# Down product of the feed-forward blocks: one step per two groups, four row tiles deep, and gate, up, gate, two down units, up as the order of the work

## The reference

```python
def swiglu(hn, w_ffn_in, w_ffn_out):
    a, b = jnp.split(hn @ w_ffn_in, 2, axis=-1)
    return (jax.nn.silu(a) * b) @ w_ffn_out
...
ff = swiglu(rmsnorm(h, norm_ffn_pre[l]), w_ffn_in[l], w_ffn_out[l])
h = h + rmsnorm(ff, norm_ffn_post[l])
```

## Time and profile before

| | |
|---|---|
| time, median of 3 runs | 1864.49 us (1863.72 to 1864.56) |
| time of the profiled execution | 1863.81 us |
| its span, first to last instruction | 1862.0 us |
| mean granted PE clock | 0.994 |
| PE busy | 1815.3 us, 97% |
| PE weight loads busy | 1626.4 us, 87% |
| DVE busy | 1335.6 us, 72% |
| ACT busy | 813.3 us, 44% |
| POOL busy | 152.8 us, 8% |
| HBM traffic | 84 GB/s over the span |

### The profile page before, as it was taken

How to read it: one execution, slowest core, us unless ns; L and a number is a source line. 1 busy time by engine, 2 the same in 40 slices (tenths; PEclk the granted TensorE clock), 3 DMA queues, 4 the chain that set the end, 5 groups by cost and what they waited for, 6 DMA issues and landing times.

```text
span 1862.0 us, 28319 instructions
## 1 busy us (share of the span) xinstructions
PE 1815.3 (97%) x11226; PEld 1626.4 (87%) x11226; DVE 1335.6 (72%) x1825; ACT 813.3 (44%) x1031; POOL 152.8 (8%) x97
## 2 busy tenths in 40 slices
PE   9999999999999999999999999999999999999996
PEld 8898989889898888988887989988898888989896
DVE  7567566753736538357678888888898778898887
ACT  5666676532322333333443333334545753343332
POOL 2000000000000000000001222220000001222210
PEclk9999999999999999999999999999999999999998
DMA  4111111132122222112412222223476312322321
GB/s 184 35 65 60 45 45 46 60 111 102 46 90 79 90 96 73 69 68 91 161 69 91 91 101 102 90 103 96 112 187 175 122 68 93 112 90 92 108 95 46
DMA packets 25989, 170.29 MB, mean 91 GB/s; under 512 B 2736, under 2 KB 5040, under 8 KB 6320
## 3 DMA queue, kind: packets, MB, share of 16 engines
q1 hardware_dynamic: 24176, 156.51, 23.5%
q0 software_dynamic: 1728, 12.58, 3.3%
HBM read 154.40 MB, written 2.10 MB: 84 GB/s over the span
## 4 chain that ended last, share of the span: by engine, by line
PE 80%; DVE 13%; issue 4%; ACT 3%; POOL 0%; DVEq 0%; ACTq 0%; POOLq 0%
PE psum L675 25%; PE psum L677 24%; PE psum L676 24%; DVE w_lo L1889 2%; DVE acc L2150 2%; DVE wx_lo L2481 1%; DVE normed L1906 1%; PE psum L826 1%; PE psum L877 1%; PE psum L872 1%; ACT w_hi L1276 1%; DVE h L1996 1%; PE psum L797 1%; ACT X_hi L1276 0%; DVE M_lo L2467 0%
## 5 line engine op out<-in xcount | busy, mean ns | idle before, releaser
L675 PE MATMUL psum<-X_hi,w_hi 128*128 128x512 f32 (+2 forms) x1392 | 467.6, 336 | 20.0 <-DVE gate_in L2549 10.9
L676 PE MATMUL psum<-X_lo,w_hi 128*128 128x512 f32 (+2 forms) x1392 | 457.9, 329 | 0.0
L677 PE MATMUL psum<-X_hi,w_lo 128*128 128x512 f32 (+2 forms) x1392 | 457.9, 329 | 0.0
L1889 DVE TENSOR_TENSOR w_lo<-w_raw,w_hi 128x2048 fp32r<-128x2048 f32 x121 | 294.9, 2438 | 59.6 <-ACT w_hi L1276 59.3
L675 PEld LDWEIGHTS psum<-X_hi,w_hi 128*128 128x128 f32 x1392 | 262.9, 189 | 54.5 <-DVE gate_in L2549 13.9
L1276 ACT ACTIVATE w_hi<-w_raw 128x2048 fp32r<-128x2048 f32 x133 | 253.5, 1906 | 119.8 <-PE psum L677 119.8
L676 PEld LDWEIGHTS psum<-X_lo,w_hi 128*128 128x128 f32 x1392 | 263.6, 189 | 25.6 <-issue 2.4
L677 PEld LDWEIGHTS psum<-X_hi,w_lo 128*128 128x128 f32 x1392 | 263.2, 189 | 23.5
L675 PE MATMUL psum<-M_hi,w_hi 128*128 128x512 f32 (+2 forms) x376 | 141.6, 377 | 0.0
L676 PE MATMUL psum<-M_lo,w_hi 128*128 128x512 f32 (+2 forms) x376 | 141.2, 376 | 0.0
L677 PE MATMUL psum<-M_hi,w_lo 128*128 128x512 f32 (+2 forms) x376 | 141.0, 375 | 0.0
(11 more groups left out here) (352 smaller groups left out, 4034.3 us busy)
## 6 DMA issues: line engine op xcount, KB each, us to landing
w_raw<-in_units SPq DMA_DIRECT2D x140, 1024.0 KB, 4.8
w_lo<-w_raw POOLq DMA_DIRECT2D x12, 1024.0 KB, 7.0
...
```

What stands on the lines that cost most here:

```text
L675: nc.tensor.matmul(dst, w2[0], x2[0], start=first, stop=False, skip_group_check=True)
L676: nc.tensor.matmul(dst, w2[0], x2[1], start=False, stop=False, skip_group_check=True)
L677: m = nc.tensor.matmul(dst, w2[1], x2[0], start=False, stop=last, skip_group_check=True)
L1889: v.tensor_tensor(lo, w_raw[at.ring(j)][:, :], as_f32(hi), ALU.subtract).then_inc(w_lo_ready, 1)
```

## The change

Groups 1 to 10 lose their own down unit. Each pair (0 and 1, 2 and 3, up to 8 and 9) gets one down step of two units of a new kind "E": 4 row tiles of 512 columns, 4 strips each of 12 matmuls 128x512. The four row tiles are the two groups' `M` slots, read as one. Only the last group keeps its "D" unit. The units are laid out in HBM in the new order. PE's order over two groups is now gate, up, gate, both down units, up (`period`); ffn1 has whole units in that order, and ffn9 has gate, up, gate, up, both down units. The tables `FF_BANKS` and `FF_REACH` name the PSUM bank of each strip and how far back the strip that last used it lies; PE waits for that one. The products that need `t4_lo` and `t3_lo` wait for them inside the first seven of a period. On DVE, `u2` and `u3` of a seven now stand ahead of the split of the next unit, and ACT makes `M_hi` between its two copies of a gate's first strip. The last hidden pair goes to `wx_hi` and `wx_lo`, free by then.

```diff
-STRIPS = {"P": 2, "R": 4, "D": 8, "S": 3}
+STRIPS = {"P": 2, "R": 4, "E": 4, "D": 8, "S": 3}
...
+FF_BANKS = {
+    "ffn0": (4, 5, 0, 1),
+    "ffn1": (2, 3, 6, 4, 5, 0, 1, 2, 3, 6, 4, 5, 0, 3, 1, 2),
+    "ffn": tuple((j + 3) % 7 for j in range(20)),
+    "ffn9": tuple((j + 3) % 7 for j in range(20)),
+}
+def reach():
+    last, far, s = {6: 3}, {}, 0
+    for phase in ("ffn0", "ffn1", "ffn", "ffn", "ffn", "ffn9"):
+        for j, bank in enumerate(FF_BANKS[phase]):
+            far[phase, j] = min(far.get((phase, j), 99), s - last[bank] if bank in last else 6)
+            last[bank] = s
+            s += 1
+    return far
+FF_REACH = reach()
 def plan():
...
-        ("ffn1", "PPDPPD"),
-        ("ffn", "SSDSSD" * 3),
-        ("ffn9", "SSDSSD"),
+        ("ffn1", "PPPEEP"),
+        ("ffn", "SSSEES" * 3),
+        ("ffn9", "SSSSEE"),
         ("ffn_end", "D"),
...
-            return (j + 2) % 7
+            return FF_BANKS[self.phase.removesuffix("_2")][j]
         return (self.turn + j) % self.depth * max(1, 4 // self.depth)
+    def before(self, j):
+        return self.strip(j) + 1 - (FF_REACH[self.phase.removesuffix("_2"), j] if self.depth == 7 else self.depth)
...
-            def two(i):
-                at = Place("ffn" + tag, i, 6, 28, 2)
-                for m in range(2):
-                    k = FIRST7 + 2 * i + m + 1
-                    first_sums(at, 3 * m + 1, index7(n, k, 0))
-                    first_sums(at, 3 * m + 2, index7(n, k, 1))
...
+            def period(i):
+                at = Place("ffn" + tag, i, 6, 20, 2)
+                k = FIRST7 + 2 * i
+                for j, (kk, c) in ((0, (1, 0)), (3, (1, 1)), (4, (2, 0)), (5, (2, 1))):
+                    first_sums(at, j, index7(n, k + kk, c))
+            loop(pool, 3, period)
...
-            def down(at, j, s, i, slot):
...
-                unit(at, j, s, "D", SEQ, lambda k, a, b: (M_hi[:, slot, k, :], M_lo[:, slot, k, :]))
-            def seven(at, j, s, idx):
+                m = seq_of(*(x[:, :, :, :].rearrange("p a b c -> p (a b) c") for x in (M_hi, M_lo)))
+                for c in range(2):
+                    unit(at, j + c, s + 4 * c, "E", SEQ, m)
...
+                if first:
+                    pe.wait_ge(t_sums.sem, t_sums.at("t4_lo", n))
                 product(r3, added_to, 0, sum_x(1), False, True, c7_pe.step("P6"))
                 taken(1)
+                if first:
+                    pe.wait_ge(t_sums.sem, t_sums.at("t3_lo", n))
...
+            def period(at, k):
+                seven(at, 0, 0, index7(n, k, 0), True)
+                seven(at, 1, 3, index7(n, k, 1))
+                seven(at, 2, 6, index7(n, k + 1, 0))
+                down(at, 3, 9, base + k)
+                seven(at, 5, 17, index7(n, k + 1, 1))
...
-            two(Place("ffn1" + tag, depth=6), 1)
-            pe.wait_ge(t_sums.sem, t_sums.at("t3_lo", n))
-            loop(pe, 3, lambda i: two(Place("ffn" + tag, i, 6, 28, 7), FIRST7 + 2 * i))
-            two(Place("ffn9" + tag, depth=7), FF_PAIRS - 2)
+            at = Place("ffn1" + tag, depth=7)
+            for j in range(3):
+                whole(at, j, 2 * j)
+            down(at, 3, 6, base + 1)
+            whole(at, 5, 14)
+            loop(pe, 3, lambda i: period(Place("ffn" + tag, i, 6, 20, 7), FIRST7 + 2 * i))
+            at = Place("ffn9" + tag, depth=7)
+            for j in range(4):
+                seven(at, j, 3 * j, index7(n, FF_PAIRS - 2 + j // 2, j % 2))
+            down(at, 4, 12, base + FF_PAIRS - 2)
...
+            def pair_and_gate(at, k, up_next, down_next):
+                strips(at, -1)
+                sums_hi(at, -1, index7(n, k, 1))
+                split_hi(at, -1)
+                gate(at, 0, k, lambda: hidden(base + k - 1, slot(up_next)))
+                strips(at, 2)
+                sums_hi(at, 0, index7(n, k + 1, 0))
+                split_hi(at, 0)
+                takes(at, 3, index7(n, k, 1), up_in, lambda: gated(k))
+                strips(at, 5)
+                if down_next:
+                    split_hi(at, 1)
+                else:
+                    sums_hi(at, 1, index7(n, k + 1, 1))
+                    split_hi(at, 1)
+                gate(at, 6, k + 1, lambda: hidden(base + k, slot(up_next + 1)))
+                strips(at, 8)
+                split_hi(at, 2)
+            def period(at, k):
+                pair_and_gate(at, k, 0, True)
+                gated(k + 1)
+                strips(at, 12)
+                sums_hi(at, 3, index7(n, k + 1, 1))
+                split_hi(at, 3)
+                strips(at, 16)
+                sums_hi(at, 4, index7(n, k + 2, 0))
+                split_hi(at, 4)
+                takes(at, 17, index7(n, k + 1, 1), up_in)
...
+            def wholes(at):
+                hidden_lo(base, *slot(0))
+                for which in ("b12", "t1", "t2", "t4"):
                     token_sums(which)
-                add_down(at, 4, range(3))
+                gates_in(at, 0)
+                split_lo(at, 0)
+                gates(base + 1)
+                token_sums("t3")
+                for t, (name, scale) in enumerate((("t1", 1.0), ("t2", -1.0), ("t4", -1.0))):
+                    token_lo(t, name, scale)
+                ups(at, 2, base + 1)
                 split_lo(at, 1)
-                hidden_lo(i, 1)
-                add_down(at, 4, range(3, 6))
-                token_sums("t4")
-                add_down(at, 4, range(6, DT))
-                token_sums("t3")
+                hidden_lo(base + 1, *slot(1))
+                gates_in(at, 4)
                 split_lo(at, 2)
-                gate_up(at, 3, 12, i + 1, between=lambda: [token_lo(t, name, scale) for t, (name, scale) in
-                                                           enumerate((("t1", 1.0), ("t2", -1.0), ("t4", -1.0)))])
+                gates(base + 2)
+                add_down(at, 6, range(4))
+                split_lo(at, 3)
+                add_down(at, 6, range(4, 6))
                 sums_of(at, 4, index7(n, FIRST7, 0))
+                add_down(at, 6, range(6, DT))
+                sums_lo(at, 4, index7(n, FIRST7, 0))
+                split_lo(at, 4)
+                sums_of(at, 5, index7(n, FIRST7, 1))
+                ups(at, 14, base + 2)
                 dve.wait_ge(t_high.sem, t_high.at("t3_hi", n))
                 v.tensor_tensor(late_half(X_lo), T3_raw, as_f32(late_half(X_hi)), ALU.subtract).then_inc(*t_sums.step("t3_lo"))
-                sums_lo(at, 4, index7(n, FIRST7, 0))
-                add_down(at, 16, range(3))
-                split_lo(at, 4)
-                sums_of(at, 5, index7(n, FIRST7, 1))
-                add_down(at, 16, range(3, 6))
-                hidden_lo(i + 1, 0)
-                sums_lo(at, 5, index7(n, FIRST7, 1))
-                add_down(at, 16, range(6, DT))
...
+            def pair_and_gate(at, k, up_next, down_next):
+                g, u, g2 = index7(n, k, 0), index7(n, k, 1), index7(n, k + 1, 0)
+                sums_lo(at, -1, u)
+                chain(at, 0, g, gate_in)
+                split_lo(at, -1)
+                corner22(at, 0, g, gate_in)
+                hidden_lo(base + k - 1, *slot(up_next))
+                sums_of(at, 0, g2)
+                gate_corners(at, 0, k)
+                sums_lo(at, 0, g2)
+                chain(at, 3, u, up_in)
+                split_lo(at, 0)
+                corner22(at, 3, u, up_in)
+                gated(k)
+                if not down_next:
+                    sums_of(at, 1, index7(n, k + 1, 1))
+                prod(at, 3, k)
+                if not down_next:
+                    sums_lo(at, 1, index7(n, k + 1, 1))
+                chain(at, 6, g2, gate_in)
+                split_lo(at, 1)
+                corner22(at, 6, g2, gate_in)
+                hidden_lo(base + k, *slot(up_next + 1))
+                gate_corners(at, 6, k + 1)
+            def period(at, k):
+                u2, g3 = index7(n, k + 1, 1), index7(n, k + 2, 0)
+                pair_and_gate(at, k, 0, True)
+                split_lo(at, 2)
+                gated(k + 1)
+                add_down(at, 9, range(2))
+                sums_of(at, 3, u2)
+                add_down(at, 9, range(2, 4))
+                sums_lo(at, 3, u2)
+                split_lo(at, 3)
+                add_down(at, 9, range(4, 6))
+                sums_of(at, 4, g3)
+                add_down(at, 9, range(6, DT))
+                sums_lo(at, 4, g3)
+                chain(at, 17, u2, up_in)
+                split_lo(at, 4)
+                corner22(at, 17, u2, up_in)
+                sums_of(at, 5, index7(n, k + 2, 1))
+                prod(at, 17, k + 1)
+            def final(at, k):
+                u2 = index7(n, k + 1, 1)
+                pair_and_gate(at, k, 0, False)
+                chain(at, 9, u2, up_in)
+                split_lo(at, 2)
+                corner22(at, 9, u2, up_in)
+                gated(k + 1)
+                prod(at, 9, k + 1)
+                split_lo(at, 3)
```

(17 more changed lines are left out.)

249 lines of the change are left out of this document (104 added, 145 removed).

## The result

The change makes the kernel faster: 1837.95 us, median of 4 runs (1837.16 to 1838.23), against 1864.36 us for the kernel before on the same chip. The profiled execution of the changed kernel took 1837.8 us with a span of 1835.6.

The account below looks back on a forecast made before the run. PE was taken to bound the kernel, with its idle time waiting for DVE to be won: 1863.81 - 21.0 + 1.5 + 0.8 = 1845.1 us; the median lies 0.7 above, so 1845.8 us, range 1841.5 to 1853.

Parts of the forecast that it names:

- idle time in reach: PE's idle time in both feed-forward blocks that waits for DVE: 16.7 + 2.7 + 1.6 = 21.0 us, all to be won.
- the list leaves out 0.16 us of each wait: PE's listed waits fall short because a matmul's recorded length overlaps the next: 17 waits x 0.16 = 2.7 us more.
- The long wait goes from 1016.09 + 0.23 to 1019.48, 3.2 us: PE's gap at the first seven; the add freeing the strip, named as second of three from 1018.75, now stands 10 us ahead.
- Adds. Alone this is worth nothing: 40 fewer adds to `acc` per block save DVE 24 us, but DVE doesn't bound; they only give the new order room.
- The order's work: New DVE order in the loop: all 15 gate `u2` waits go; margins 1.4 and 1.0 us in first gate, 0.5 and 0.3 in up.
- The charges, 1.5 us for ffn9 and 0.8 for the start of the sevens: Losses added back: 0.75 us per block in peeled ffn9 (bounds 0, 2.6), 0.4 per block at the first seven (0, 2.6).
- the lock: Two-SBUF-input DVE ops and POOL ops exclude each other, first come first served; without it the sum is 1.5 us better.
- The argument against B: The second POOL op overlaps DVE steps that read PSUM and were not stretched: `u2` stays 0.41.
- B: Tight first up of a period gives part back: `c22` 0.5 to 2 us late at 8 places, 1850 to 1862 us; chance 0.17.
- E: More is won: uncounted losses under 0.12 us go too, 1841 to 1843 us; chance 0.03.
- C: The waits only move, to `M_lo` or a strip of the four-deep product: 1861 to 1868 us; chance 0.05.
- D: Slower: three sevens in a row overload DVE, 8 x 3.0 = 24 us lost against 21 won, 1868 us; chance 0.05.

Follow-up runs that it names:

- b_start: Kernel before, with the eight adds ahead of each block's first seven replaced by one-column copies that free the strips: 1861.63 us.
- b_start_ahead: Kernel before, eight adds ahead of first seven left out, `w_lo` behind next gate's `u2` and `u3`, strips 3 to 5 freed before DVE's waiting weight sum: 1839.94 us.
- b_noadds: Kernel before, with every second add of a down step to `acc` replaced by a one-column copy, 40 fewer per block, DVE's order kept: 1843.22 us.
- b_order: Kernel before, with only `w_lo` of the next up moved behind the next gate's `u2` and `u3` in DVE's queue: 1846.98 us.
- a_gated: Changed kernel, with the two products of the gate (1.2 us) put ahead of `c22` in the first up of each two groups: 1847.50 us.

## Why the prediction was right or wrong

**What bounds, and the idle time in reach: right in kind, too small in size.** PE bound, and what was won is its idle time. The three kinds of loss that the prediction counted are 21.1 us in the table, forecast 21.0, and all but 0.4 went. But PE's idle time was 28.0 us, since two terms stood at nothing. The step "the list leaves out 0.16 us of each wait" stopped one matmul early: the second matmul after a wait starts 0.1 us late too. 3.1 us of that before, 0.6 after.

**"The long wait goes from 1016.09 + 0.23 to 1019.48, 3.2 us": mis-sized.** The gap had a tail at half the granted clock, for which the sum had no term. It cost 1.5 and 2.4 us in the profiled execution, 3.9 in sum. The windows of the earlier trace rows already gave a clock of 0.99 where a block without it has 1.00; I did not follow that 0.01. I also named the wrong add: the first of the three from 1018.75 freed the strip, as it ends 0.1 us before PE starts; the sum does not depend on it. And the cause was not the add's place alone but what it stood behind (b_start, b_start_ahead). In the kernel before itself DVE worked without a pause from 1010.75 to this add, and a `w_lo` in it took 3.28 us.

**"Adds. Alone this is worth nothing": wrong.** b_noadds won 20.9 us with them alone. The sum did not suffer, since order and adds remove the same waits.

**The order's work: right.** b_order won 17.1 us. The margins laid out from rows of before against those measured: first gate 1.4 and 1.0 us against 1.4 and 1.1; the up behind it 0.5 and 0.3 against 0.9 and 0.8. The up is the tightest, as said, but my 0.3 was 0.5 too small.

**The charges, 1.5 us for ffn9 and 0.8 for the start of the sevens: too high.** PE lost 0.4 us in each ffn9, at the second gate's `u2` and `c22` as said, where 0.75 were charged, and nothing at the start. `X_lo` is ready 0.35 us before PE's third product, forecast 0.3. For the lock I had taken the case in which DVE pays ahead of `c22`; in the change POOL pays there, or DVE in `M_lo` and the products, which stand behind it. POOL's 26.5 us more busy time are that. The lock still reaches PE in ffn9: in its first up `w_lo` (1218.78) takes 2.83 us and the two products 2.05 instead of 1.29, 1.3 us more in an unbroken chain of DVE up to the late `u2` (1228.95). The argument against B named a row that overlaps no sum of POOL, the `u2` of the earlier trace rows; the changed kernel bears it out, with `c22` at 1086.34 taking 0.42 us during POOL's sum.

**The sum.** It failed in three terms. Of the 8.3 us by which the 27.0 of the table exceed the forecast's 18.7, the stretch at half clock is 3.9, the second matmuls 3.1 - 0.6 = 2.5, and the charges 2.3 - 0.4 = 1.9. The later start of the first block brought it back to 26.4.

**The rivals.** E, more is won, had the right sign with 0.03 and one cause that was too small, the losses under 0.12 us. B, C and D did not occur. But a_gated shows that B's place was real: 1.2 us more ahead of `c22` in that up cost 9.5 us, the slow matmuls behind it included.
